# Gate and up products of a feed-forward block, pair by pair in Strassen's scheme

## The chip, the cores and the metric

The kernel runs on one core of one Trainium2 chip. The metric is device time in microseconds (us); the kernel before has a median of 2981.46 us in 3 runs (2981.38 to 2981.63). TensorE (PE) multiplies, VectorE (DVE), ScalarE (ACT) and GpSimd (POOL) do the elementwise work, SyncE (SP) issues the loads of the weights.

## What is computed

Two hybrid layers (convolution, retention, window attention) are followed by one block of another kind, over 512 tokens and a model width of 1024, in float32. The change is in the last stretch of that block:

```
h1 = layer_norm(ALPHA * h + mix)
hid = silu(h1 @ w_ffn_gate) * (h1 @ w_ffn_up)        # 1024 -> 2816, twice
ffn = hid @ w_ffn_down                               # 2816 -> 1024
ple = sigmoid(h1 @ w_ple_gate + b) * (p @ w_ple)
h = layer_norm(ALPHA * h1 + ffn + ple)
```

## The kernel before

Activations lie transposed: 128 features on the partitions, 512 tokens along a row. A float32 product is made of three: each operand is split in a high part (rounded to fp32r) and a low part (the rest), and PE adds high x high, high x low and low x high. Weights come as one stream of slabs of 128x1024, eight tiles of 128x128: for a product of width 1024 the eight tiles that make one tile of 128 outputs. For each slab SP loads it into one of two `raw` buffers, ACT copies it to `whi` (L984, four slots), POOL subtracts in two halves to get `wlo` (L325), and PE makes 8 tiles x 3 terms = 24 matmuls of 512 columns into one bank of `gem` (L392 to L394). POOL's low part frees the raw buffer, PE's last matmul of a slab (`slab_done`) frees the slot.

After the second layer norm (ACT writes the normed rows to `yr`, DVE and ACT the parts `hhi`, `hlo`) comes the per-layer embedding ("PLE"): 8 slabs whose products ACT passes through a sigmoid, and which DVE multiplies by `PL` (L2516) and adds to ALPHA x `yr` in `cv` (L2518).

The feed-forward block has 22 tiles of 128 hidden features in groups of 8, 8 and 6 (`FF_GROUPS`). For each tile the gate slab and the up slab follow each other, a "pair". ACT takes the gate product out of PSUM with Silu (L993), DVE multiplies it by the up product (L2528) and splits the result into `zhi` and `zlo` (L1669 the cast, L1671 the subtraction). After a group come 8 slabs of the down projection (one for each output tile, with as many tiles as the group has pairs), and DVE adds each product to `cv` (L2538). The order of each engine is written out by hand and held together by counting semaphores; every engine executes its own list in order.

## Time and profile before

| | us |
|---|---|
| median of 3 runs | 2981.46 |
| the profiled execution's own time | 2982.7 |
| its span, first to last instruction | 2980.9 |
| PE busy | 2957.1 (99%) |
| DVE, ACT, POOL busy | 1751.4, 1194.3, 1415.5 |

Of PE's 14216 matmuls most have 512 columns. The profile shows 389 ns for one, but they are pipelined, and the distance from start to start tells what they cost. The layer norm before the changed stretch ends near 2577 us, the embedding's slabs near 2607, and the feed-forward matmuls near 2966.

### The profile page before, as it was taken

What the parts mean: (1) busy time and instruction counts of PE and PEld (TensorE: products, weight loads), DVE (VectorE), ACT (ScalarE), POOL (GpSimd) and SP (SyncE); (2) the same over time, 40 slices, a digit from 0 to 9 for tenths busy, and PEclk for the clock granted to TensorE, in tenths of its full rate; (3) what the DMA queues carried; (4) which work ended last, traced back from release to release, by engine and by line L of the source; (5) the groups of instructions that cost most, each with busy time, mean ns of one, the idle gap of its engine ahead of it and who ended that gap; (6) DMA issues with size and microseconds to landing.
All of it is one profiled execution on the core that took longest, in us unless ns stands there. A gap on an engine that the chain in (4) does not pass through costs nothing.

```text
span 2980.9 us, 41951 instructions
## 1 busy us (share of the span) xinstructions
PE 2957.1 (99%) x14216; PEld 2432.5 (82%) x14216; DVE 1751.4 (59%) x2640; ACT 1194.3 (40%) x1820; POOL 1415.5 (47%) x1040
## 2 busy tenths in 40 slices
PE   8999999999999999999999999999999999999998
PEld 6888888878888888888887888888888888788886
DVE  7985677874524598568688644377773343611214
ACT  4233333484332424333347633246553323522223
POOL 5443443455555443443355545544343544554544
PEclk9999999999999999999999999999999999999999
DMA  4322222212223332222221222232222323223222
GB/s 152 99 71 74 95 77 83 88 44 100 92 99 101 121 99 85 85 84 74 81 92 51 86 97 95 97 113 73 76 77 92 107 85 119 94 96 99 98 93 91
DMA packets 73849, 271.06 MB, mean 91 GB/s; under 512 B 8192, under 2 KB 9088, under 8 KB 73088
## 3 DMA queue, kind: packets, MB, share of 16 engines
q1 hardware_dynamic: 70560, 254.84, 26.1%
q10 hardware_dynamic: 3168, 14.61, 1.3%
q8 instruction: 76, 1.25, 0.2%
q14 instruction: 45, 0.37, 0.0%
HBM read 264.17 MB, written 5.24 MB: 90 GB/s over the span
## 4 chain that ended last, share of the span: by engine, by line
PE 86%; issue 7%; POOL 5%; DVE 1%; ACT 1%; DVEq 0%; DMA 0%; POOLq 0%; ACTq 0%; SPq 0%
PE gem L392 19%; PE gem L394 19%; PE gem L393 19%; POOL wlo L325 5%; PE gem L827 2%; PE gem L829 2%; PE gem L828 2%; PE gem L518 2%; PE gem L517 2%; PE gem L519 2%; PE gem L637 2%; PE gem L639 1%; PE gem L638 1%; PE gem L663 1%; PE xp L681 1%
## 5 line engine op out<-in xcount | busy, mean ns | idle before, releaser
L325 POOL TENSOR_TENSOR wlo<-raw,whi 128x512 fp32r<-128x512 f32 x956 | 1320.4, 1403 | 1532.9 <-ACT whi L984 1532.8
L984 ACT ACTIVATE whi<-raw 128x1024 fp32r<-128x1024 f32 x478 | 504.2, 1056 | 667.4 <-PE gem L394 490.8
L392 PE MATMUL gem<-zhi,whi 128*128 128x512 f32 x1664 | 649.1, 390 | 0.3 <-DVE zlo L1671 0.3
L394 PE MATMUL gem<-zhi,wlo 128*128 128x512 f32 x1664 | 647.6, 389 | 0.0
L393 PE MATMUL gem<-zlo,whi 128*128 128x512 f32 x1664 | 647.4, 389 | 0.0
L392 PE MATMUL gem<-hhi,whi 128*128 128x512 f32 x1280 | 498.7, 390 | 0.0
L394 PE MATMUL gem<-hhi,wlo 128*128 128x512 f32 x1280 | 498.0, 389 | 0.0
L393 PE MATMUL gem<-hlo,whi 128*128 128x512 f32 x1280 | 498.0, 389 | 0.0
L392 PEld LDWEIGHTS gem<-zhi,whi 128*128 128x128 f32 x1664 | 312.4, 188 | 65.5 <-DVE zlo L1671 0.8
L394 PEld LDWEIGHTS gem<-zhi,wlo 128*128 128x128 f32 x1664 | 312.3, 188 | 65.3
L393 PEld LDWEIGHTS gem<-zlo,whi 128*128 128x128 f32 x1664 | 312.4, 188 | 64.5
L394 PEld LDWEIGHTS gem<-hhi,wlo 128*128 128x128 f32 x1280 | 240.2, 188 | 50.3
L392 PEld LDWEIGHTS gem<-hhi,whi 128*128 128x128 f32 x1280 | 240.3, 188 | 50.0 <-issue 0.2
L393 PEld LDWEIGHTS gem<-hlo,whi 128*128 128x128 f32 x1280 | 240.3, 188 | 49.8
L993 ACT ACTIVATE U<-gem 128x512 f32<-128x512 f32 x118 | 70.3, 596 | 297.1 <-PE gem L394 271.9
L1887 DVE SCALAR_TENSOR_TENSOR xp<-cv,sm,xp 128x512 f32<-128x512 f32 x224 | 158.6, 752 | 16.2 <-issue 13.9
L993 ACT ACTIVATE U<-gem,vec 128x512 f32<-128x512 f32 x96 | 65.6, 685 | 237.1 <-PE gem L394 215.9
L1826 DVE SCALAR_TENSOR_TENSOR xp<-cv,vec,xp 128x512 f32<-128x512 f32 x208 | 147.8, 752 | 9.0 <-issue 0.4
L2528 DVE TENSOR_TENSOR U<-gem,U 128x512 f32<-128x512 f32 x22 | 15.2, 692 | 185.5 <-PE gem L394 185.5
L827 PE MATMUL gem<-zhi,whi 128*128 128x512 f32 x256 | 106.5, 416 | 0.7 <-POOL wlo L325 0.7
L1993 DVE TENSOR_TENSOR yr<-gem,yr 128x512 f32<-128x512 f32 x64 | 41.2, 685 | 101.8 <-PE gem L394 101.8
L829 PE MATMUL gem<-zhi,wlo 128*128 128x512 f32 x256 | 100.2, 391 | 0.0
(451 smaller groups left out, 4344.9 us busy)
## 6 DMA issues: line engine op xcount, KB each, us to landing
raw<-in_slabs SPq DMA_DIRECT2D x478, 512.0 KB, 3.4
U<-in_x SPq DMA_DIRECT2D x4, 512.0 KB, 6.8
U<-in_x ACTq DMA_DIRECT2D x1, 2048.0 KB, 9.6
xsave<-U ACTq DMA_DIRECT2D x1, 2048.0 KB, 7.1
U<-xsave ACTq DMA_DIRECT2D x1, 2048.0 KB, 9.8
out_y<-yr SPq DMA_DIRECT2D x8, 256.0 KB, 2.2
tab<-in_tab_ret ACTq DMA_DIRECT2D x2, 512.0 KB, 5.1
tab<-in_tab_att ACTq DMA_DIRECT2D x2, 512.0 KB, 3.5
```

Of the source, the lines that this page charges most:

```text
L325: part = pool.tensor_tensor(wlo[:, k % 4, c], raw[:, k % 2, c], whi[:, k % 4, c].bitcast(f32), O.subtract)
L392: pe.matmul(o, wh, hi, start=(n == 0), stop=False)
L393: pe.matmul(o, wh, lo, start=False, stop=False)
L394: mm = pe.matmul(o, wl, hi, start=False, stop=(n == len(terms) - 1))
L517: pe.matmul(o, hhi[:, k, c], wh, start=(k == 0), stop=False)
L518: pe.matmul(o, hhi[:, k, c], wl, start=False, stop=False)
L827: pe.matmul(gem[:, k, :], wh, hhi[:, r, :], start=(r == 0), stop=False)
L829: mm = pe.matmul(gem[:, k, :], wl, hhi[:, r, :], start=False, stop=(r == NT - 1))
L984: act.activation(whi[:, k % 4, :], raw[:, k % 2, :], A.Copy).then_inc(hi_done, 1)
L993: act.activation(dst, gem[:, b, :], func, bias=bias, scale=scale).then_inc(evac[b], 1)
L1826: stt(held if n < TAPS - 1 else TT[:, 0, :], v, w, acc, O.mult, O.add)
L1887: stt(acc if n < TAPS - 1 else TT[:, 0, :], v, w, acc, O.mult, O.add)
```

## The change

The two slabs of a pair are seen as a matrix of 2x2 blocks: A11 and A12 are the gate's four tiles over the lower and the upper half of the 1024 features, A21 and A22 the up slab's. The activations are four blocks too: lower and upper features by the first and last 256 tokens. Strassen's scheme in Winograd's form makes the four block products with 7 multiplications in place of 8. Each is 4 tiles x 3 terms = 12 matmuls of 256 columns, 84 for a pair in place of 48 of 512.

- Weights: DVE makes four sums of 128x512 for each pair (`sums`: S1 = A21 + A22, S2 = S1 - A11, S4 = A12 - S2, S3 = A11 - A21), two pairs ahead of PE. ACT makes the high part of the 7 blocks in half slots of 512 columns, 8 of them; POOL makes the low part of 5 (`BY_POOL`), DVE of S1 and S3 (`low_half`).
- Activations: DVE makes four differences of 128x1024 once, out of `yr` (`lessen`), ACT and DVE split them. ALPHA x `yr` is written to `cv` beforehand, and the embedding adds to it.
- Results: products land in halves of four banks for a pair, alternating between even and odd pairs. Three products each add onto an earlier one in PSUM. ACT copies four halves of 256 tokens out, DVE makes four sums of 256 tokens with one operand in PSUM (`early` makes the gate's first 256 tokens, `late` the rest), ACT applies Silu from SBUF, and DVE multiplies and splits as before.
- PE waits for `early` of a pair before it adds S2 into the bank (`f_added`), for ACT's copies before S4 and S3 (`f_kept`), and for `late` two pairs back before a bank is used again.
- Loads go to four buffers instead of two in this stretch; the down slabs are converted in halves. The loops are written out. DVE makes the sums for a group's first two pairs while the down products of the group before run.

```diff
+N_PLAIN = 4 * (BLOCK_G + PLE) + 10
+PAIRS = sum(FF_GROUPS)
+STARTS = (0, 8, 16)
+A11, A12, S1, A22, S2, S4, S3 = range(7)
+BY_POOL = (A11, A12, A22, S2, S4)
...
+        RAWS = (raw[:, 0, :], raw[:, 1, :], U[:, U_T + 2 * T:U_T + 4 * T], U[:, U_VF:U_VF + 2 * T])
+        flat_tab = tab[:, :, :].rearrange("p a b -> p (a b)")
+        SUM = ((flat_tab[:, 0:T], flat_tab[:, T:2 * T], U[:, U_C:U_C + T], U[:, U_C + T:U_C + 2 * T]),
+               tuple(U[:, U_C + n * T:U_C + (n + 1) * T] for n in range(2, 6)))
+        HALF = T // 2
+        KEPT5, KEPT2 = ([U[:, U_C + (6 + e) * T + n * HALF:U_C + (6 + e) * T + (n + 1) * HALF] for e in range(2)]
+                        for n in range(2))
+        GATE = [U[:, U_SG + (2 + e) * T:U_SG + (3 + e) * T] for e in range(2)]
...
+        DIFF_HI, DIFF_LO = ([quads(t) for t in (
+            Ur[:, at:at + 2 * T], yr_r[:, at:at + 2 * T],
+            yr_r[:, 4 * T + at:6 * T + at], Ur[:, 4 * T + at:6 * T + at])] for at in (0, 2 * T))
+        def half_slot(t, j):
+            n = (4 + j) % 8
+            return t[:, n // 2, n % 2 * T:(n % 2 + 1) * T]
...
-            lows(at, N_SLABS)
+            lows(at, N_PLAIN)
+            def low_half(j, src):
+                pool.wait_ge(f_hi, j + 1)
+                pool.tensor_tensor(half_slot(wlo, j), src, half_slot(whi, j).bitcast(f32), O.subtract).then_inc(f_lo, 1)
+            for g, n in enumerate(FF_GROUPS):
+                for p in range(STARTS[g], STARTS[g] + n):
+                    for m in BY_POOL:
+                        low_half(unit(p, m), source(p, m))
+                for i in range(NT):
+                    for h in range(2):
+                        low_half(unit_out(g, i, h), raw_out(g, i, h))
...
-            m0, z0 = 0, Z0 + 24
-            for n in FF_GROUPS:
-                with pe.Fori(0, n // 2) as it:
-                    for k in range(2, 6):
-                        hslab(Gp + (it + (2 + m0 // 4)), k, up + (it + (4 + m0 // 4)), k0=2)
-                m0 += 2 * n
+            def pair_product(p, m, o, hi, lo, opens=False):
+                j = unit(p, m)
+                if m in BY_POOL:
+                    pe.wait_ge(f_lo, pool_low(p, m))
+                else:
+                    pe.wait_ge(f_own, own_low(p, m))
+                for r in range(4):
+                    wh, wl = (half_slot(w, j)[:, r * P:(r + 1) * P] for w in (whi, wlo))
+                    pe.matmul(o, wh, hi[:, r, :], start=(opens and r == 0), stop=False, skip_group_check=True)
+                    pe.matmul(o, wh, lo[:, r, :], start=False, stop=False, skip_group_check=True)
+                    mm = pe.matmul(o, wl, hi[:, r, :], start=False, stop=(r == 3), skip_group_check=True)
+                mm.then_inc(f_free, 1)
+            def pair(p):
+                g, x, y = p // 8, 2 * (p % 2), 2 * (p % 2) + 1
+                ca, cb, cc, cd = xp[:, x, 0:HALF], gem[:, x, 0:HALF], xp[:, y, 0:HALF], gem[:, y, 0:HALF]
+                t1, t2 = slice(0, HALF), slice(HALF, T)
+                if p >= 2:
+                    pe.wait_ge(f_added, added(p - 2, 2))
+                pair_product(p, A11, ca, hhi[:, 0:4, t1], hlo[:, 0:4, t1], True)
+                if p % 8 < 2:
+                    pe.wait_ge(evac[x], up + 4 + 2 * g + PRIMED)
+                pair_product(p, A12, cb, hhi[:, 4:8, t1], hlo[:, 4:8, t1], True)
+                if p == 0:
+                    pe.wait_ge(f_diff, 9)
+                pair_product(p, S1, cc, DIFF_HI[0], DIFF_LO[0], True)
+                if p % 8 < 2:
+                    pe.wait_ge(evac[y], up + 4 + 2 * g + PRIMED)
+                pair_product(p, A22, cd, DIFF_HI[3], DIFF_LO[3], True)
+                pe.wait_ge(f_added, added(p, 0))
+                pair_product(p, S2, ca, DIFF_HI[1], DIFF_LO[1])
+                pe.wait_ge(f_kept, kept(p, 1))
+                pair_product(p, S4, cc, hhi[:, 4:8, t2], hlo[:, 4:8, t2])
+                pe.wait_ge(f_kept, kept(p, 3))
+                pair_product(p, S3, ca, DIFF_HI[2], DIFF_LO[2])
...
+            def high_half(j, src, arrived):
+                if j >= 8:
+                    act.wait_ge(f_free, j - 7)
+                else:
+                    act.wait_ge(slab_done, N_PLAIN - 4 + j // 2 + 1 + PRIMED)
+                arrived()
+                act.activation(half_slot(whi, j), src, A.Copy).then_inc(f_hi, 1)
...
+                    for m in range(7):
+                        if m == A12:
+                            act.wait_ge(f_free, unit(p, A12) + 1)
+                            if p < 2:
+                                act.wait_ge(sg_used, 8 + PRIMED)
+                            act.activation(GATE[e][:, 0:HALF], gem[:, 2 * e, 0:HALF], A.Copy).then_inc(f_kept, 1)
+                        if m == S1:
+                            act.wait_ge(f_free, unit(p, S1) + 1)
+                            if p >= 2:
+                                act.wait_ge(f_added, added(p - 2, 2))
+                            act.activation(KEPT5[e], y[:, 0:HALF], A.Copy).then_inc(f_kept, 1)
+                        if m == A22:
+                            act.wait_ge(f_free, unit(p, A22) + 1)
+                            if p == 0:
+                                act.wait_ge(f_sum, 4)
+                            else:
+                                act.wait_ge(z_ready, DEPTH * 40 + 24 + p + PRIMED)
+                            act.activation(TT[:, 0, 0:HALF], gem[:, 2 * e + 1, 0:HALF], A.Copy).then_inc(f_kept, 1)
+                        if m == S2:
+                            act.wait_ge(f_free, unit(p, S2) + 1)
+                            act.activation(KEPT2[e], x[:, 0:HALF], A.Copy).then_inc(f_kept, 1)
+                        if m == S3:
+                            act.wait_ge(f_added, added(p, 1))
+                            if p >= 2:
+                                act.wait_ge(z_ready, DEPTH * 40 + 24 + p - 1 + PRIMED)
+                            act.activation(SGB[:, e, :], GATE[e], A.Silu).then_inc(f_kept, 1)
+                        ahead(g, n, 7 * (p - STARTS[g]) + m + 8)
...
+            def lessen(n, x, y):
+                return tt(DIFF[n], x, y, O.subtract)
+            first, second = (slice(n * HALF, (n + 1) * HALF) for n in range(2))
+            lessen(0, yr[:, 0:4, second], yr[:, 0:4, first])
+            lessen(2, yr[:, 4:8, second], yr[:, 0:4, second])
+            dve.drain()
+            lessen(1, yr[:, 4:8, second], DIFF[0]).then_inc(f_diff, 1)
+            dve.drain()
+            lessen(3, yr[:, 4:8, first], DIFF[1]).then_inc(f_diff, 1)
+            for i in range(0, NT, 4):
+                ts(cv[:, i:i + 4, 0:T], yr[:, i:i + 4, :], ALPHA, None, O.mult)
+            dve.drain().then_inc(f_diff, 3)
...
+            def sums(p, ms):
+                a, b = (RAWS[PLACE[load_of(p, n)]] for n in range(2))
+                for m in ms:
+                    if m == S1:
+                        for n in range(2):
+                            loaded(dve, load_of(p, n))
+                        if p >= 2:
+                            dve.wait_ge(f_lo, pool_low(p - 2, S4))
+                        op = tt(sum_of(p, S1), b[:, 0:T], b[:, T:2 * T], O.add)
+                    elif m == S2:
+                        dve.drain()
+                        op = tt(sum_of(p, S2), sum_of(p, S1), a[:, 0:T], O.subtract)
+                    elif m == S4:
+                        dve.drain()
+                        op = tt(sum_of(p, S4), a[:, T:2 * T], sum_of(p, S2), O.subtract)
+                    else:
+                        op = tt(sum_of(p, S3), a[:, 0:T], b[:, 0:T], O.subtract)
+                    op.then_inc(f_sum, 1)
+            def low_half(p, m):
+                j = unit(p, m)
+                dve.wait_ge(f_hi, j + 1)
+                tt(half_slot(wlo, j), sum_of(p, m), half_slot(whi, j).bitcast(f32), O.subtract).then_inc(f_own, 1)
+            def diff_low(at, n):
+                dve.wait_ge(f_dhi, at + 1)
+                tt(DIFF_LO[n], DIFF[n], DIFF_HI[n].bitcast(f32), O.subtract).then_inc(f_diff, 1)
...
-                stt(cv[:, i, 0:T], yr[:, i, :], ALPHA, TT[:, k % 2, :], O.mult, O.add)
+                tt(cv[:, i, 0:T], cv[:, i, 0:T], TT[:, k % 2, :], O.add)
                 dve.drain()
-            m0, z0 = 0, 0
-            for n in FF_GROUPS:
-                with dve.Fori(0, n // 2) as it:
-                    G, u = Gp + (it + (2 + m0 // 4)), up + (it + (4 + m0 // 4))
-                    for k in (3, 5):
-                        product(G, k)
-                        dve.wait_ge(evac[(k - 1) % 4], u + 1 + PRIMED)
-                        j = (k - 3) // 2
-                        tt(TT[:, j, :], gem[:, k % 4, :], SGB[:, j, :], O.mult).then_inc(evac[k % 4], 1)
-                        dve.drain()
-                        split(zhi[:, it * 2 + j, :], zlo[:, it * 2 + j, :], TT[:, j, :], z_ready)
-                        dve.drain()
-                m0 += 2 * n
+                if 4 <= k < 8:
+                    diff_low(k - 4, (0, 3, 1, 2)[k - 4])
+                if k == 7:
+                    sums(0, (S1, S2, S4, S3))
+                if k == 8:
+                    low_half(0, S1)
+            sums(1, (S1, S2, S4, S3))
+            low_half(0, S3)
...
+            def early(p):
+                e = p % 2
+                x = xp[:, 2 * e, :]
+                dve.wait_ge(f_kept, kept(p, 0))
+                tt(GATE[e][:, first], x[:, first], GATE[e][:, first], O.add).then_inc(f_added, 1)
+            def late(p, following):
+                e = p % 2
+                x, y = xp[:, 2 * e, :], xp[:, 2 * e + 1, :]
+                dve.wait_ge(f_free, unit(p, S4) + 1)
+                dve.wait_ge(f_kept, kept(p, 3))
+                tt(GATE[e][:, second], KEPT2[e], y[:, first], O.add).then_inc(f_added, 1)
+                dve.wait_ge(f_free, unit(p, S3) + 1)
+                tt(TT[:, 0, first], x[:, first], TT[:, 0, first], O.add)
+                tt(TT[:, 0, second], x[:, first], KEPT5[e], O.add).then_inc(f_added, 1)
+                if following:
+                    low_half(p + 1, S3)
+                dve.drain()
+                dve.wait_ge(f_kept, kept(p, 4))
+                tt(TT[:, 1, :], TT[:, 0, :], SGB[:, e, :], O.mult)
+                dve.drain()
+                split(zhi[:, p % 8, :], zlo[:, p % 8, :], TT[:, 1, :], z_ready)
+                dve.drain()
+            for g, n in enumerate(FF_GROUPS):
+                last = STARTS[g] + n - 1
+                for p in range(STARTS[g], last + 1):
+                    early(p)
+                    if p + 2 <= last:
+                        sums(p + 2, (S1, S2))
+                    if p + 1 <= last:
+                        low_half(p + 1, S1)
+                    if p + 2 <= last:
+                        sums(p + 2, (S4, S3))
+                    late(p, p + 1 <= last)
```

## Rows read from the trace of the kernel before

**Rows 1.** Page, parts 1 and 2: TensorE's busy time, and its granted clock in 40 slices.
```profile
PE 2957.1 (99%) x14216; PEld 2432.5 (82%) x14216; DVE 1751.4 (59%) x2640; ACT 1194.3 (40%) x1820; POOL 1415.5 (47%) x1040
PEclk9999999999999999999999999999999999999999
```

**Rows 2.** Page, part 4: the chain that ended last, by engine.
```profile
PE 86%; issue 7%; POOL 5%; DVE 1%; ACT 1%; DVEq 0%; DMA 0%; POOLq 0%; ACTq 0%; SPq 0%
```

**Rows 3.** Windows, first pairs: busy us of PE, PEld, DVE, ACT, POOL; granted clock.
```profile
2608.00:2695.00 87.00, 87.00 (x386) 72.03 (x385) 17.98 (x25) 22.44 (x26) 43.76 (x32) 1.00 0.31 100
```

**Rows 4.** Timeline (start us, us, engine, line, operation) of PE, matmuls of 512 columns.
```profile
2694.02 0.39 PE L394 MATMUL gem<-hhi,wlo 128*128 128x512 f32 x1
2696.06 0.39 PE L394 MATMUL gem<-hhi,wlo 128*128 128x512 f32 x1
```

**Rows 5.** Timeline of PE, attention scores, matmuls of 256 columns.
```profile
587.25 0.28 PE L663 MATMUL gem<-zhi,zlo 64*128 64x256 f32 x2
587.72 0.28 PE L663 MATMUL gem<-zlo,zhi 64*128 64x256 f32 x2
```

**Rows 6.** Timeline of PE's weight loads in the HGRN stage.
```profile
2036.84 1.99 PEld L836 LDWEIGHTS xp<-U 128*128 128x128 f32 x16
```

**Rows 7.** Groups by line, shapes apart, 2550 to 2980.9 us: busy us, mean ns, idle before.
```profile
L325 POOL TENSOR_TENSOR wlo<-raw,whi 128x512 fp32r<-128x512 f32 x152 | 208.9, 1394 | 199.1 <-ACT whi L984 199.1
L984 ACT ACTIVATE whi<-raw 128x1024 fp32r<-128x1024 f32 x75 | 79.4, 1058 | 175.8 <-PE gem L394 158.7 <-DMA raw<-in_slabs 16.9 <-PE gem L952 0.2
L993 ACT ACTIVATE U<-gem 128x512 f32<-128x512 f32 x26 | 15.5, 595 | 91.5 <-PE gem L394 91.5
```

**Rows 8.** Timeline of DVE: one pair of the loop before.
```profile
2650.25 0.69 DVE L2528 TENSOR_TENSOR U<-gem,U 128x512 f32<-128x512 f32 x1 [7.78 <-PE gem L394]
2651.13 0.43 DVE L1669 CAST hhi<-U 128x512 f32 x1 [0.19 <-issue]
2651.71 0.69 DVE L1671 TENSOR_TENSOR hlo<-U,hhi 128x512 f32 x1
```

**Rows 9.** Timeline of DVE: gating products of the per-layer embedding.
```profile
2578.99 0.69 DVE L2516 TENSOR_TENSOR U<-U 128x512 f32<-128x512 f32 x1 [3.93 <-ACT U L993]
2579.78 0.69 DVE L2518 SCALAR_TENSOR_TENSOR cv<-yr,U 128x512 f32<-128x512 f32 x1
2580.55 1.63 DVE L2516 TENSOR_TENSOR U<-U 128x512 f32<-128x512 f32 x1
...
2585.66 1.60 DVE L2518 SCALAR_TENSOR_TENSOR cv<-yr,U 128x512 f32<-128x512 f32 x1
```

**Rows 10.** Timeline of POOL beside them, and alone.
```profile
2579.88 6.83 POOL L325 TENSOR_TENSOR wlo<-raw,whi 128x512 fp32r<-128x512 f32 x4 [7.75 <-ACT whi L984]
...
2609.87 2.54 POOL L325 TENSOR_TENSOR wlo<-raw,whi 128x512 fp32r<-128x512 f32 x2 [3.54 <-ACT whi L984]
```

**Rows 11.** Timeline: DVE with a PSUM input (xp) and without, beside POOL.
```profile
2569.13 3.00 POOL L325 TENSOR_TENSOR wlo<-raw,whi 128x512 fp32r<-128x512 f32 x2 [5.67 <-ACT whi L984]
2569.36 0.68 DVE L1728 SCALAR_TENSOR_TENSOR U<-xp,U 128x512 f32<-128x512 f32 x1
2569.97 1.01 DVE L1751 SCALAR_TENSOR_TENSOR zlo<-U,vec,zhi 128x512 fp32r<-128x512 f32 x1
```

**Rows 12.** Groups by line, shapes apart, DVE: a subtraction of 1024 columns.
```profile
L1938 DVE TENSOR_TENSOR hlo<-xp,hhi 128x1024 fp32r<-128x1024 f32 x8 | 9.8, 1225 | 8.8 <-ACT hhi L1161 8.8
```

**Rows 13.** Timeline of PE near the start, around a wait.
```profile
15.65 0.50 PE L477 MATMUL gem<-zhi,whi 128*128 128x512 f32 x1 [1.50 <-DVE zlo L1777]
...
18.24 0.63 PE L477 MATMUL gem<-zhi,whi 128*128 128x512 f32 x1
18.67 0.63 PE L478 MATMUL gem<-zlo,whi 128*128 128x512 f32 x1
```

**Rows 14.** Timeline of ACT: last normed rows, last gate of the embedding.
```profile
2574.18 2.55 ACT L1038 ACTIVATE yr<-U,vec 128x512 f32<-128x512 f32 x4
...
2606.73 0.69 ACT L993 ACTIVATE U<-gem,vec 128x512 f32<-128x512 f32 x1 [3.00 <-PE gem L394]
```

More of the change, by code:

```diff
@@ new lines, in down @@
+            def down(g, n, i):
+                bank = (2 + i) % 4
+                o = gem[:, bank, :]
+                pe.wait_ge(evac[bank], up + 4 + 2 * g + i // 4 + PRIMED)
+                for h in range(2):
+                    j = unit_out(g, i, h)
+                    pe.wait_ge(f_lo, pool_out(g, i, h))
+                    for r in range(4 * h, min(4 * h + 4, n)):
+                        if i == 0:
+                            pe.wait_ge(z_ready, Z0 + 24 + STARTS[g] + r + 1 + PRIMED)
+                        wh, wl = (half_slot(w, j)[:, (r - 4 * h) * P:(r - 4 * h + 1) * P] for w in (whi, wlo))
+                        pe.matmul(o, wh, zhi[:, r, :], start=(r == 0), stop=False)
+                        pe.matmul(o, wh, zlo[:, r, :], start=False, stop=False)
+                        mm = pe.matmul(o, wl, zhi[:, r, :], start=False, stop=(r == n - 1))
+                    mm.then_inc(f_free, 1)
@@ L963, in _ @@
+            for g, n in enumerate(FF_GROUPS):
+                for p in range(STARTS[g], STARTS[g] + n):
+                    pair(p)
                 for i in range(NT):
-                    zslab(Gp + (2 + m0 // 4) + i // 4, 2 + i % 4, up + (4 + m0 // 4) + i // 4,
-                          (z_ready, z0 + PRIMED) if i == 0 else None, n, k0=2)
-                    if z0 + n == Z0 + 24 + sum(FF_GROUPS) and i == 2:
+                    down(g, n, i)
+                    if g == 2 and i == 2:
                         mean_sum(3)
-                m0, z0 = m0 + 8, z0 + n
@@ L1643, in _ @@
                     log_exp()
[L1644 to L1646 removed]
+                for i in range(NT):
+                    for h in range(2):
+                        ahead(g, n, 7 * n + 2 * i + h + 8)
+                    if g == 2:
                         for j in LN_TURNS[i]:
                             centered(3, j, cv[:, j, 0:T])
[L1649 removed]
             shifted_root(3)
```

134 lines of the change are left out of this document (108 added, 26 removed).

## The prediction

> **What bounds the kernel now.** I read the page's busy line first, then the chain, and then the feed-forward stretch by windows, groups and timelines. TensorE is busy 99% of the span at full clock [rows 1], and the chain that ended last is 86% PE work [rows 2]. In the first group of pairs (2608 to 2695 us) PE has no idle time; POOL is busy 43.8 of 87 us, ACT 22.4 and DVE 18.0 [rows 3]. So the stretch costs what PE streams. Nine matmuls of 512 columns start 2.04 us apart [rows 4], 226.7 ns each. A pair (gate slab and up slab) has 48 of them: 10.88 us. Twenty-two pairs are 239.4 us; the down products (about 120 us) stay.
>
> **What it makes of PE.** 7 products x 4 tiles x 3 terms are 84 matmuls of 256 columns per pair. The nearest rows are the attention scores, also split in three terms, 256 columns wide but with 64 rows of the array: four starts span 0.47 us [rows 5], 117.5 ns each. A pair is then 9.87 us, a product 1.41. Below, half of 226.7 ns gives 9.5 us; above, 16 loads of 128x128 weights in a row take 1.99 us [rows 6], 0.124 each, and if loading sets the pace 10.4 us. I take 9.87 because its shape is nearest: 22 x 1.01 = 22 us less, if PE is never kept waiting. The Trainium skill (TensorE: Matmul & The Clock Gate, Back-to-back issue gap) gives N/2.4 + 2.5 ns warm, 109 ns here and 9.2 us a pair; the 512-column row (226.7 against its 216) is slower than that, so I don't use it.
>
> **What it adds elsewhere, per full pair.** POOL: 5 differences of 128x512 instead of 4; alone each takes 1.27 (2.54 for two) [rows 10], 6.35 us of 9.9. ACT: 7 high halves at about 0.6 (1.06 for 1024 columns), 4 copies of 256 at 0.4, one Silu 0.6 [rows 7]: 6.4 us; it fits, but executes in order. DVE had 1.8 us of work in 10.9. Now it has:
> - 8 tensor_tensor of 512 with both inputs in SBUF (4 weight sums, 2 low halves, gate x up, low part of z), 0.69 each alone [rows 8, 9]: 5.52
> - the cast of z: 0.43 [rows 8]
> - 4 sums of 256 with one input in PSUM: 512 columns take 0.69 [rows 8] and 1024 take 1.225 [rows 12], so 256 take 0.42: 1.68
> - 13 gaps after drains and waits, 0.08 to 0.19 in [rows 8, 9], 0.1 taken: 1.3
>
> That is 8.9 us, already 90% of PE's new pair. On top of it comes POOL. When both are busy, DVE's operations with two SBUF inputs take 1.59 to 1.63 instead of 0.69, and POOL's four take 6.83 instead of 5.08 [rows 9, 10]: they alternate, 1.7 us for one of each. With an input in PSUM DVE is not slowed (0.68 beside a running POOL operation), with two in SBUF it is (1.01) [rows 11]. So each POOL operation can cost DVE up to 0.92. The Trainium skill (SBUF — State Buffer, Who interferes with whom) says that a DVE instruction with two SBUF inputs contends with a GpSimd one that reads SBUF, under an exclusive lock; the rows agree, and by this rule the change turns a PE-bound stretch into a DVE/POOL-bound one, which is my forecast.
>
> **One steady pair by hand.** t=0 is the end of product S3 of pair p on PE. DVE: two 256 sums to 0.9. ACT converts A11 of p+2, POOL takes it 0.75 to 1.95; DVE's low half of S3 waits and ends at 2.55. POOL has the next (A12) 2.5 to 3.7; gate x up ends 4.3, cast 4.9, z's low part 5.75; POOL holds 5.7 to 6.9 (A22), beside which early(p+1), with PSUM input, ends at 6.3. Only now may PE start S2 of p+1, for which it was ready at 5.65. Then sums, one low half, two sums and a 256 sum meet POOL's S2 and S4: DVE is through at 12.95, while S2, S4 and S3 on PE ended at 10.5. In the next round ACT's Silu and the highs behind it start late and I get 13.4. The bounds for this cycle T: with no collisions PE's 9.87; with PE kept by early but the rest hidden 6.5 + 4.24 = 10.7; all five collisions at full price 8.9 + 4.6 = 13.5. I take 8.9 + 5 x 0.8 = 12.9 (a collision is cheaper where a PSUM sum lies beside POOL).
>
> **A group.** sums() runs two pairs ahead, so the last two pairs have none. First A11 to early of pair 1: 9.9 + 6.9 = 16.8. Then n-3 cycles of T. Then S2, S4, S3 (4.25) and the tail to the last early (6.9), and 4.25 for the last three products. That is 32.2 + (n-3)T. Over 8, 8 and 6 pairs: 96.6 + 13T = 264.3 at T=12.9, against 239.4: +24.9.
>
> **The start.** DVE gets new work between the layer norm and the pairs. yr is complete at 2576.7 (ACT's last four end there [rows 14]). Then 4 differences of 1024 (1.23 each by [rows 12]) and 2 scalings of 2048 (1.2 each if as fast per element as the cast, 2.3 if not): 7.9 with gaps. Then 8 rounds of 1.58 for the gating, 4 low parts at 1.33, 8 weight sums at 0.79, 2 low halves at 0.8: 25.8. The sum ends at 2610.4 without POOL. POOL runs some 15 operations meanwhile (a pair each 4 to 5.4 us), about 12 us of collisions: 2622.7. PE would need early(0) 5.65 us after the end of the gating products (ACT reads the last at 2606.7 [rows 14]), at 2612.3. So +10, with bounds 0 and 15. ACT is in order too: its read of bank 0 stands behind the high half of S1, which waits for DVE's sums, and PE's A12 waits for that bank.
>
> **The ends of groups.** The down products need the last z 4.8 us (6 pairs: 3.4) after they start; late of the last pair takes about 3.3 + 1.6. +2 in all. Raw tiles come earlier and into 4 buffers; the DMAs have no part in the bound. The old loop's bank traffic hid under PE and its removal gives nothing.
>
> **Sum.** 24.9 + 10 + 2 = +37 on the profiled execution's 2982.7 (span 2980.9 and 1.8 around it); the median of the three runs is 1.2 lower: 2981.5 + 37 = 3018.
>
> **Rivals.**
> - PE stays the bound: if DVE and POOL rarely meet and T is 9.87, the pairs give -22 and the start costs up to 5: 2959 to 2966, 2961 taken. For it: POOL is only 64% busy of such a pair, and its operations are released one by one by products. Against it: DVE's own 8.9 us leave 1 us for five operations of 1.27. It decides below T = 10.1, where 13T - 130.8 crosses zero. By the skill's 109 ns it would be 15 us better still.
> - They collide at half price: the loop through early and S3, T about 10.7, start +6, ends +1: 96.6 + 139 - 239.4 + 7 = +3, so 2985.
> - The clock. The new pair leaves PE idle some 3 us at a stretch. Near the start, 2.6 us after a wait of 1.5 us, matmuls of 512 columns came 0.43 apart [rows 13], the level of 1.2 GHz. A product then costs up to 2.56. If each of the 16 cycles after a group's second pair has such a stretch in S2, S4 and S3, hidden in part, I put 1.5 us on each: +24 on the forecast, 3042. For it: the row. Against it: one idle stretch, at a cold start; in the full cycle DVE's 6.6 us after early cover 4.24 and most of the loss.
>
> **How the numbers follow.** Forecast 65% (its own range T 11.8 to 13.5, start 5 to 15: 2999 to 3033), PE-bound 10%, half price 10%, clock 15%. The range reaches from half price to past the clock: 2986 to 3046. A measurement here can tell 0.2% (6 us) from no change. Faster by more: 0.10. Within: half of the half-price case and a little of the forecast's tail, 0.07. Slower: 0.83.
>
> **What would show it.** PE busy about 80% in the pair stretches, with waits whose releaser is DVE (early, or own low halves). DVE at 90% or more there, its two-SBUF operations at 1.1 to 1.3 mean; POOL's at 1.4 to 1.6. PE 256-column starts 118 ns apart inside a product. Seven-product cycles 12.9 apart in the middle of a group and 11 at its end. PE idle about 10 us around the first pair. I am wrong if PE has no waits on DVE in the pairs, if two-SBUF operations stay near 0.69, or if the 256-column start distance is above 130 ns, where Strassen's scheme gives nothing even with PE alone.

## The result, and the profile after

The kernel before took 2981.42 us (median of 4 runs, 2981.35 to 2981.63), the changed one 3023.76 us (4 runs, 3022.31 to 3025.42): ratio 1.0142, 95% interval 1.0124 to 1.016. The change costs 42 us; 37 were forecast. The profiled execution took 3024.92 us, 42.2 more than the one of before (2982.7).

First the page, parts 1 and 2 (busy us of each engine; granted clock in 40 slices), against [rows 1], then part 4, the chain's shares, against [rows 2]:
```profile
PE 2960.4 (98%) x15008; PEld 2472.8 (82%) x15008; DVE 1968.7 (65%) x2870; ACT 1274.2 (42%) x2046; POOL 1466.5 (49%) x1062
...
PEclk9999999999999999999999999999999999999999
...
PE 78%; issue 7%; DVE 6%; POOL 5%; DVEq 2%; ACT 1%; DMA 0%; POOLq 0%; ACTq 0%; SPq 0%
```
DVE has 217 us more, POOL 51, ACT 80. PE's busy time did not fall (2957.1 before), although each pair streams less: part of its matmuls ran slower (below), which 40 wide slices do not show. The chain has lost eight points of PE, and DVE has gained five.

What PE waited for, over the whole span (engine, line, releaser: us in total, times, longest). The lines of the feed-forward block are L1120 (pairs) and L1161 (down):
```profile
PE xp L1120 <- DVE U L2843: 31.2, 13, 3.0
...
PE xp L1120 <- DVE wlo L2813: 3.6, 1, 3.6
PE gem L1120 <- ACT U L1197: 2.2, 1, 2.2
PE gem L1161 <- DVE hlo L1934: 1.0, 1, 1.0
```
L2843 is `early`: 13 times, up to 3.0 us, PE's S2 stands behind the addition of DVE that frees its bank. That is 31.2 of the 38.0 us that PE waits in the feed-forward block.

Windows of the first pairs and of five pairs inside the second group (busy us of PE, PEld, DVE, ACT, POOL; granted clock; DMA share; GB/s), against [rows 3]:
```profile
2606.16:2731.00 124.84, 104.59 (x742) 99.83 (x741) 98.44 (x111) 56.27 (x110) 74.59 (x51) 0.93 0.29 92
2779.28:2846.34 67.06, 57.84 (x423) 56.82 (x421) 54.84 (x65) 29.67 (x61) 37.00 (x25) 0.87 0.26 79
```
In the second window PE is busy 86%, DVE 82%, POOL 55%, and the granted clock is 0.87: no engine is full. Its pairs start at 2779.28, 2795.13, 2805.45, 2820.18, 2830.5 and 2846.34, so they take 10.3 and 14.7 to 15.9 us in turn. Three of the five are long ones, so their mean of 13.4 us is above the kernel's own. Taken on DVE from one `early` to the next, the 13 cycles between a group's second pair and its last but one take 11.8 to 13.2 us, 12.73 on the mean.

DVE's timeline through one of them (start us, us, engine, line, operation [idle before, releaser]), against [rows 8]:
```profile
2787.69 0.42 DVE L2843 TENSOR_TENSOR U<-xp,U 128x256 f32<-128x256 f32 x1
2788.03 0.68 DVE L2798 TENSOR_TENSOR tab<-raw 128x512 f32<-128x512 f32 x1
2788.81 1.69 DVE L2801 TENSOR_TENSOR tab<-tab,raw 128x512 f32<-128x512 f32 x1
...
2793.70 0.42 DVE L2851 TENSOR_TENSOR U<-U,xp 128x256 f32<-128x256 f32 x1 [1.22 <-PE xp L1122]
2795.33 0.42 DVE L2853 TENSOR_TENSOR U<-xp,U 128x256 f32<-128x256 f32 x1 [1.21 <-PE xp L1122]
...
2796.78 1.61 DVE L2859 TENSOR_TENSOR U<-U 128x512 f32<-128x512 f32 x1
```
POOL's timeline in the same place:
```profile
2788.67 1.27 POOL L512 TENSOR_TENSOR wlo<-U,whi 128x512 fp32r<-128x512 f32 x1 [1.62 <-ACT whi L1830]
```
The operation with two SBUF inputs takes 0.68 alone and 1.69 beside POOL's. In this long pair DVE also waits twice, 1.2 us each, for products that PE did late.

PE's timeline around the first wait for `early` shows why such products are late, against [rows 5] and [rows 13]:
```profile
2606.27 0.28 PE L1121 MATMUL xp<-zlo,whi 128*128 128x256 f32 x1
2606.39 0.28 PE L1122 MATMUL xp<-zhi,wlo 128*128 128x256 f32 x1
...
2623.85 0.58 PE L1120 MATMUL xp<-yr_r,whi 128*128 128x256 f32 x1 [2.78 <-DVE U L2843]
2624.23 0.42 PE L1121 MATMUL xp<-yr_r,whi 128*128 128x256 f32 x1
2624.45 0.41 PE L1122 MATMUL xp<-yr_r,wlo 128*128 128x256 f32 x1
...
2626.79 0.28 PE L1121 MATMUL xp<-zlo,whi 128*128 128x256 f32 x1
2626.91 0.28 PE L1122 MATMUL xp<-zhi,wlo 128*128 128x256 f32 x1
```
Windows, after that wait (same columns as above, granted clock 0.50):
```profile
2624.20:2626.70 2.50, 2.50 (x13) 2.50 (x13) 2.32 (x4) 0.00 (x0) 0.39 (x1) 0.50 0.84 295
```
At full clock 256-column matmuls start 0.12 us apart. After the wait of 2.78 us they start 0.213 apart, the level of 1.2 GHz, and are back at 0.12 by 2626.8. In the block 187 distances are of the slow kind, 187 x 0.094 = 17.5 us of PE time.

A group of POOL and two of DVE, 2570 us to the end (x count, busy us, mean ns, idle before), against [rows 7, 8]:
```profile
L512 POOL TENSOR_TENSOR wlo<-U,whi 128x512 fp32r<-128x512 f32 x82 | 119.7, 1473 | 89.4 <-ACT whi L1830 89.4
...
L2859 DVE TENSOR_TENSOR U<-U 128x512 f32<-128x512 f32 x22 | 36.6, 1663 | 2.0
...
L1932 DVE CAST hhi<-U 128x512 fp32r<-128x512 f32 x23 | 28.5, 1240 | 1.7
```
The product gate x up meets POOL every time (1663 ns against 690), and the cast of z nearly every time (1240 on the mean, 430 alone).

Where the 42 us are: the first pair takes 23.3 us on PE where 9.9 would do (+13.4). The three groups take 280.3 together; without that loss at the start they take 266.9, against 239.4 before (+27.5). The first down product waits 1.0. The sum is 41.9.

### The profile page after: what moved, and what is told of

Its sections match the earlier page's. It is cut to its first block, busy times and chain, and to the rows that moved or that the text cites. A ratio compares the mean times of both kernels' runs of the same rounds, so it can differ in the third digit from the quotient of the medians.

```text
span 3023.1 us, 43745 instructions
## 1 busy us (share of the span) xinstructions
PE 2960.4 (98%) x15008; PEld 2472.8 (82%) x15008; DVE 1968.7 (65%) x2870; ACT 1274.2 (42%) x2046; POOL 1466.5 (49%) x1062
## 3 DMA queue, kind: packets, MB, share of 16 engines
q1 hardware_dynamic: 70560, 254.84, 27.5%
## 4 chain that ended last, share of the span: by engine, by line
PE 78%; issue 7%; DVE 6%; POOL 5%; DVEq 2%; ACT 1%; DMA 0%; POOLq 0%; ACTq 0%; SPq 0%
PE gem L545 14%; PE gem L547 14%; PE gem L546 14%; POOL wlo L465 5%; PE gem L980 2%; PE gem L982 2%; PE gem L981 2%; PE gem L672 2%; PE gem L670 2%; PE gem L671 2%; PE gem L790 2%; PE gem L792 1%; PE gem L791 1%; PE gem L1161 1%; PE gem L1163 1%
## 5 line engine op out<-in xcount | busy, mean ns | idle before, releaser
L465 POOL TENSOR_TENSOR wlo<-raw,whi 128x512 fp32r<-128x512 f32 x820 | 1137.3, 1409 | 1358.1 <-ACT whi L1188 1358.0
L1188 ACT ACTIVATE whi<-raw 128x1024 fp32r<-128x1024 f32 x410 | 432.2, 1056 | 494.3 <-PE gem L547 328.6
L545 PE MATMUL gem<-zhi,whi 128*128 128x512 f32 x1312 | 512.2, 390 | 0.3 <-DVE zlo L1934 0.3
L547 PE MATMUL gem<-zhi,wlo 128*128 128x512 f32 x1312 | 510.8, 389 | 0.0
L546 PE MATMUL gem<-zlo,whi 128*128 128x512 f32 x1312 | 510.6, 389 | 0.0
L545 PE MATMUL gem<-hhi,whi 128*128 128x512 f32 x1104 | 430.3, 390 | 0.0
L547 PE MATMUL gem<-hhi,wlo 128*128 128x512 f32 x1104 | 429.7, 389 | 0.0
L546 PE MATMUL gem<-hlo,whi 128*128 128x512 f32 x1104 | 429.6, 389 | 0.0
L547 PEld LDWEIGHTS gem<-zhi,wlo 128*128 128x128 f32 x1312 | 246.3, 188 | 51.6
L2150 DVE SCALAR_TENSOR_TENSOR xp<-cv,sm,xp 128x512 f32<-128x512 f32 x224 | 158.5, 752 | 16.2 <-issue 13.9
L512 POOL TENSOR_TENSOR wlo<-U,whi 128x512 fp32r<-128x512 f32 x82 | 119.7, 1473 | 89.4 <-ACT whi L1830 89.4
L512 POOL TENSOR_TENSOR wlo<-raw,whi 128x512 fp32r<-128x512 f32 x65 | 98.2, 1524 | 68.0 <-ACT whi L1830 67.9
L980 PE MATMUL gem<-zhi,whi 128*128 128x512 f32 x256 | 106.5, 416 | 0.7 <-POOL wlo L465 0.7
```

Of the source, the lines that this page charges most:

```text
L465: part = pool.tensor_tensor(wlo[:, k % 4, c], raw[:, k % 2, c], whi[:, k % 4, c].bitcast(f32), O.subtract)
L512: pool.tensor_tensor(half_slot(wlo, j), src, half_slot(whi, j).bitcast(f32), O.subtract).then_inc(f_lo, 1)
L545: pe.matmul(o, wh, hi, start=(n == 0), stop=False)
L546: pe.matmul(o, wh, lo, start=False, stop=False)
L547: mm = pe.matmul(o, wl, hi, start=False, stop=(n == len(terms) - 1))
L980: pe.matmul(gem[:, k, :], wh, hhi[:, r, :], start=(r == 0), stop=False)
```

## The experiments

Theory A: DVE and POOL share a resource, and what they do for a pair does not fit into PE's 9.9 us, by the sum of DVE's work and POOL's hold on it. Theory B: the loop through `early` (PE's S3, DVE's work up to `early`, PE's S2) sets the cycle, however much DVE does in all. Theory C: the half clock after waits makes the cost. Theory D: 256-column matmuls are too dear. Where nothing else is said, the edit is to the changed kernel. Each run is compared with runs of the kernel before on the same chip (medians 2981.42 to 2981.54).

**e1_pool_writes: POOL without reads.**
```diff
-                        low_half(unit(p, m), source(p, m))
+                        pool.wait_ge(f_hi, unit(p, m) + 1)
+                        pool.memset(half_slot(wlo, unit(p, m)).bitcast(f32), 0.0).then_inc(f_lo, 1)
```


> POOL writes zeros into the five low parts of a pair in place of subtracting (the low parts of these weight blocks are left out), so it reads nothing from SBUF there; all else is as in the changed kernel (3023.8). If POOL's reads on the shared side are what lengthens DVE's tail (DVE's two-SBUF operations 0.69 in the pairs, early in time), the ten waits of 3 us for early and the half clock after them go: pairs near PE's own 10.1 us, start still 6 to 13 us late, 2974 to 2984. If DVE's own work of 8.9 us or the loop of dependences bounds without POOL: above 3000. If the 256-column matmuls themselves are too slow: no change but the start, above 3010.

Measured 2971.35 us, ratio 0.9968 (0.9955 to 0.998), some 3 us under the range expected. Windows of five pairs:
```profile
2641.00:2690.60 49.60, 48.53 (x411) 48.33 (x410) 33.74 (x56) 29.07 (x59) 19.21 (x26) 1.00 0.35 106
```
DVE's timeline in one of them, then POOL's:
```profile
2642.14 0.69 DVE L2860 TENSOR_TENSOR U<-U 128x512 f32<-128x512 f32 x1
2642.90 0.71 DVE L1933 CAST hhi<-U 128x512 fp32r<-128x512 f32 x1
...
2646.20 0.69 DVE L2814 TENSOR_TENSOR wlo<-tab,whi 128x512 fp32r<-128x512 f32 x1
```
```profile
2642.80 0.53 POOL L518 MEMSET wlo<- 128x512 f32 x1 [0.90 <-ACT whi L1831]
2645.95 0.53 POOL L518 MEMSET wlo<- 128x512 f32 x1 [2.62 <-ACT whi L1831]
```
A pair is 9.92 us, PE is full and its clock 1.00. DVE does all it did, in 6.7 us of 9.9. With POOL not reading, the change gains 10 us instead of losing 42: 52 us hang on its five subtractions. The two-SBUF operation beside a writing POOL (2646.20) keeps its 0.69; the cast does not (0.71 against 0.43).

**e2_small_sums: DVE's four weight sums over 8 columns, POOL untouched.**
```diff
-                        op = tt(sum_of(p, S1), b[:, 0:T], b[:, T:2 * T], O.add)
+                        op = tt(sum_of(p, S1)[:, 0:8], b[:, 0:8], b[:, T:T + 8], O.add)
...
```
S2, S4 and S3 are cut in the same way.

> The four weight sums of a pair are made over 8 of their 512 columns (the rest of S1 to S4 is stale data), which takes about 2.1 us of DVE's work out of each full pair, and their collisions. If DVE's total per pair is the bound: most of the loss goes, 2975 to 2990. If the bound is the way from the end of product S3 through late's tail to early of the next pair, in which no sums stand, the waits for early stay at 2 to 3 us in every second pair and only the start gets shorter: 3008 to 3018.

Measured 2980.89 us, 0.9998 (0.9988 to 1.0007). Between the first and the last of a group pairs take 10.32 us, and the listed waits for `early` are only 3.9 us in all:
```profile
PE xp L1120 <- DVE U L2843: 3.9, 4, 1.1
PE xp L1120 <- DVE wlo L2813: 3.1, 1, 3.1
PE gem L1120 <- ACT U L1197: 1.6, 1, 1.6
```
The loop of theory B has no weight sum in it, and it was untouched, yet the long waits went. So B alone falls: the sum of DVE's work decides when `early` comes, because DVE is in order. But what is left is B's loop: in each of these pairs DVE waits 0.1 us for S3's product and PE 0.3 us for `early`, and the loop closes at 10.32 us. The short pairs of the changed kernel have the same length. By itself, with POOL beside it, the loop costs 0.4 us a pair over PE's 9.92.

**e3_filler: 16 matmuls ahead of the wait for early, to keep PE at work.**
```diff
+                pe.wait_ge(f_kept, kept(p, 0))
+                for r in range(16):
+                    pe.matmul(gem[:, x, t2], ones_r[:, :], hhi[:, 0, t1], start=True, stop=True,
+                              skip_group_check=True)
```


> Before PE waits for early, 16 matmuls of 256 columns go into an unused half bank (1.9 us of extra PE work a pair, 42 us in all). If the half clock after each 3 us wait is a good part of the loss, it goes where the idle time falls near 1 us: S2, S4, S3 take 4.3 in place of up to 7.1, and though pairs without a wait become longer, the total is at most 3025, at best 3010. If the clock is nothing but a by-product of waiting, the filler adds up to 1.9 us in each pair that had no wait: 3035 to 3045.

Measured 3019.34 us (3019.26 to 3019.35), 1.0127 (1.011 to 1.0144): 4.4 us less than the changed kernel, though the filler is 1.9 us a pair (pairs that PE bounds take 11.8 us instead of 9.92). Six pairs in the first group, by windows:
```profile
2627.16:2701.41 74.25, 72.13 (x602) 70.95 (x601) 68.01 (x77) 36.05 (x73) 42.62 (x30) 1.00 0.28 86
```
One cycle of DVE in it, timeline:
```profile
2647.05 0.42 DVE L2847 TENSOR_TENSOR U<-xp,U 128x256 f32<-128x256 f32 x1
2647.39 0.68 DVE L2802 TENSOR_TENSOR tab<-raw 128x512 f32<-128x512 f32 x1
2648.16 1.70 DVE L2805 TENSOR_TENSOR tab<-tab,raw 128x512 f32<-128x512 f32 x1
2649.79 0.68 DVE L2817 TENSOR_TENSOR wlo<-U,whi 128x512 fp32r<-128x512 f32 x1
2650.56 1.61 DVE L2808 TENSOR_TENSOR U<-raw,tab 128x512 f32<-128x512 f32 x1
...
2654.46 1.75 DVE L2863 TENSOR_TENSOR U<-U 128x512 f32<-128x512 f32 x1
2656.29 1.36 DVE L1936 CAST hhi<-U 128x512 fp32r<-128x512 f32 x1
2657.73 1.63 DVE L1938 TENSOR_TENSOR hlo<-U,hhi 128x512 fp32r<-128x512 f32 x1
2659.45 0.42 DVE L2847 TENSOR_TENSOR U<-xp,U 128x256 f32<-128x256 f32 x1
```
The clock is 1.00 and the cycles even: early to early 12.40 us, 2647.05 to 2659.45, and DVE waits for nothing in it: there are six gaps of 0.07 to 0.09 us, and the other operations overlap a little. This is DVE's own time T with POOL beside it. Five of its operations are long, one for each of POOL's: 1.70, 1.61, 1.75 and 1.63 against 0.69, and 1.36 against 0.43. That is 4.86 us, 0.97 each. Theory C can hold for the rest only. The changed kernel's 13 steady cycles, 12.73 us on the mean, are 0.33 longer than this 12.40. The last cycle of a group differs more: 12.8, 13.9 and 14.0 us there, 11.3 here.

**e4_act_keeps: early's place.** ACT copies A11's product away, so that S2 waits for ACT, and early adds A12's product from PSUM.
```diff
-                pe.wait_ge(f_added, added(p, 0))
+                pe.wait_ge(f_kept, kept(p, 0))
+                pe.wait_ge(f_added, added(STARTS[g] + n - 1, 0))
-                            act.activation(GATE[e][:, 0:HALF], gem[:, 2 * e, 0:HALF], A.Copy).then_inc(f_kept, 1)
+                            act.activation(GATE[e][:, 0:HALF], x[:, 0:HALF], A.Copy).then_inc(f_kept, 1)
-                tt(GATE[e][:, first], x[:, first], GATE[e][:, first], O.add).then_inc(f_added, 1)
+                tt(GATE[e][:, first], gem[:, 2 * e, first], GATE[e][:, first], O.add).then_inc(f_added, 1)
```


> ACT copies A11's product (the one that PE adds onto) out of PSUM in place of A12's, and DVE's early adds A12's from PSUM, so that PE's S2 waits for ACT's copy and not for DVE. The computation is the same. If the wait for early is the bound (a dependence, with DVE idle 1.2 and 1.2 us later in the same pair): the 3 us waits go, and T falls from 13.1 to DVE's busy time and gaps, 11.5 to 12: 2998 to 3008. If DVE's total is the bound already: 3016 to 3024.

Measured 3010.21 us, 1.0099 (1.0082 to 1.0116), between the two ranges expected. The wait for `early` is gone, and another has its place:
```profile
PE xp L1120 <- ACT U L1899: 25.6, 15, 2.4
```
PE now waits for ACT's copy of A22, which itself stands behind DVE's last z. Steady cycles are 12.56 us, still DVE without a wait. With DVE full, a wait taken from one product turns up at the next. The 13.5 us gained come with fewer slow matmuls, 91 distances at half clock instead of 187, and lie mostly outside the steady cycles: 4 us in the first pair and more in the last cycles of the groups (9.2 to 10.5 us instead of 12.8 to 14.0).

**e5_before_256: the kernel before, its gate and up slabs in two passes of 256 columns.** The number of matmuls doubles, the columns stay.
```diff
+                        for c in (slice(0, T // 2), slice(T // 2, T)):
+                            for r in range(NT):
+                                o = gem[:, k % 4, c]
+                                pe.matmul(o, wh, hhi[:, r, c], start=(r == 0), stop=False)
...
```


> The kernel before, with the matmuls of the 44 gate and up slabs made in two passes of 256 columns (96 for a pair in place of 48 of 512), nothing else changed. It prices the narrow matmul without any of Strassen's additions: at the 0.118 to 0.120 us of the scores and of the changed kernel's undisturbed products a pair takes 11.3 to 11.5 us in place of 10.88, so 22 pairs add 10 to 14 us: 2991 to 2996. If the narrow matmul is itself a large part of the 42 us (0.13 us each and more with both halves of the weights loaded anew): above 3010.

Measured 2995.67 us (2995.63 to 2995.68), 1.0046 (1.0029 to 1.0063): +14.2 us. Over 22 pairs that is 10.88 + 0.64 = 11.52 a pair of 96 matmuls, 0.120 each. At 0.120 Strassen's 84 take 10.1, and e1's pairs took 9.92. Theory D falls: 0.8 to 1.0 of the 1.01 us a pair are there if PE is never kept waiting.

**e6_all_dve: all seven low parts on DVE, POOL idle in the pairs.**
```diff
-                for p in range(STARTS[g], STARTS[g] + n):
-                    for m in BY_POOL:
-                        low_half(unit(p, m), source(p, m))
...
+                    if p + 1 <= last:
+                        low_half(p + 1, A12)
+                        low_half(p + 1, A22)
...
```


> The changed kernel with all seven low parts of a pair made by DVE, none by POOL (POOL keeps the down slabs). The computation is the same. Theory: DVE is the bound, and a POOL operation costs it about 0.88 us of waiting, more than the 0.77 (operation and gap) of doing it itself. Then T falls from 12.4 (no half clock) to 11.8, and the total from 3024 to 3005 to 3017. Rival: sharing the work with POOL helps, and DVE with 5 x 0.77 = 3.9 us more of its own needs 13 to 15 a pair: 3035 to 3060.

Measured 2983.93 us, 1.0006 (0.9996 to 1.0015): 40 us less than the changed kernel, and far under what I had expected. Windows inside the second group:
```profile
2770.00:2800.00 30.00, 29.26 (x246) 28.85 (x245) 28.54 (x52) 16.88 (x35) 0.00 (x0) 1.00 0.33 104
```
Four lines of DVE's cycle there:
```profile
2775.99 0.69 DVE L2858 TENSOR_TENSOR U<-U 128x512 f32<-128x512 f32 x1
...
2782.96 0.69 DVE L2798 TENSOR_TENSOR U<-U 128x512 f32<-128x512 f32 x1
2783.56 0.69 DVE L2805 TENSOR_TENSOR wlo<-tab,whi 128x512 fp32r<-128x512 f32 x1
...
2786.54 0.69 DVE L2858 TENSOR_TENSOR U<-U 128x512 f32<-128x512 f32 x1
```
The cycle is 10.55 us (2775.99 to 2786.54) with 13 two-SBUF operations instead of 8, and DVE is still the bound (28.54 of 30). Such operations in a row start 0.60 to 0.61 apart, though one lasts 0.69. So DVE's work without POOL's five is 10.55 - 5 x 0.61 = 7.5 us, and a subtraction on POOL costs DVE (12.40 - 7.5) / 5 = 0.98 us, one done by DVE itself 0.61. The expectation had both wrong in the same direction.

**e7_more: e6, and three dependences moved to ACT** (A11's product kept by ACT as in e4; the copy of A22 into a buffer of its own for each parity; the cast of z).
```diff
-                            act.activation(TT[:, 0, 0:HALF], gem[:, 2 * e + 1, 0:HALF], A.Copy).then_inc(f_kept, 1)
+                            act.activation(part[:, e * HALF:(e + 1) * HALF], gem[:, 2 * e + 1, 0:HALF], A.Copy).then_inc(f_kept, 1)
-                split(zhi[:, p % 8, :], zlo[:, p % 8, :], TT[:, 1, :], z_ready)
+                act.activation(Z[DEPTH][0][:, p % 8, :], TT[:, 1, :], A.Copy).then_inc(f_cast, 1)
+                tt(zlo[:, p % 8, :], TT[:, 1, :], zhi[:, p % 8, :].bitcast(f32), O.subtract).then_inc(z_ready, 1)
```


> e6, and three dependences and one operation less on DVE: ACT keeps A11's product so that PE's S2 doesn't wait for DVE; ACT copies A22's product into a place of its own per parity, so that it doesn't wait for the last z; ACT makes the cast of z, DVE only its low part. The computation is the same. If DVE's sum is the bound: 11.8 less 0.43 and a gap, T = 11.3, no long waits and no half clock: 2993 to 3003. If waits in a loop are the bound and not the sum: T near 10.1, 2978 to 2988.

Measured 2971.05 us, 0.9962 (0.9948 to 0.9976), below both ranges expected, which had started from T = 11.8 for e6. Pairs take 9.92 us and PE waits for nothing in them: PE is the bound again, and the scheme pays. DVE's cycle is close behind: 9.88 us in the first group, where it waits for nothing either. What is left are waits at the start (pair 0 takes 13.7, pair 1 12.7).

**e8_shadow: e7, S4's low part on POOL, released so that it lies beside sums with a PSUM input.**
```diff
+                    pool.wait_ge(f_own, own_low(p, S2))
+                    low_half(unit(p, S4), source(p, S4))
```


> e7, with one low part a pair (S4) back on POOL, released when DVE goes over to its three sums with a PSUM input (1.2 us in which DVE doesn't need what they share). If a POOL operation beside PSUM sums is free, T is 0.77 less than in e7, near 10.5 and close to PE's 10.1: 2981 to 2993. If POOL's operation costs DVE as much wherever it lies: as e7 within 3 us or slower.

Measured 2971.10 us, 0.9964 (0.995 to 0.9978), as e7. Since PE is the bound in both, the time tells nothing about what the POOL operation costs DVE there, but the trace does. DVE's timeline, then POOL's:
```profile
2653.21 0.41 DVE L2866 TENSOR_TENSOR U<-xp,U 128x256 f32<-128x256 f32 x1
2653.54 1.02 DVE L2819 TENSOR_TENSOR wlo<-U,whi 128x512 fp32r<-128x512 f32 x1
```
```profile
2652.71 1.30 POOL L513 TENSOR_TENSOR wlo<-U,whi 128x512 fp32r<-128x512 f32 x1 [8.32 <-DVE wlo L2819]
```
The sums with a PSUM input keep their 0.41 to 0.42 us beside POOL, and only the low part behind them is longer, 1.02 instead of 0.68. In the first group, where DVE waits in neither kernel, its cycle is 9.62 us against e7's 9.88. So in this place POOL's subtraction costs DVE 0.33 us, a third of the 0.98 elsewhere and less than the 0.61 of DVE's doing it.

**e9_act_scales: e7, and the residual's two scalings ahead of the pairs by ACT instead of DVE.**
```diff
+                    act.activation(cv[:, i:i + 4, 0:T], yr[:, i:i + 4, :], A.Copy, scale=ALPHA)
-                ts(cv[:, i:i + 4, 0:T], yr[:, i:i + 4, :], ALPHA, None, O.mult)
```


> e7 (2971.1), and ALPHA x yr is written to cv by ACT in two pieces before its first two gate reads, in place of DVE's two scalings (4.5 us of DVE in e7). The computation is the same. Of the 55 us in which DVE works off its new work at the start, PE loses 6 to 7 us around the first two pairs. If DVE's backlog is what PE waits for there, 3 to 4 us of it go: 2966.5 to 2969. If the wait is ACT's order (the high halves stand behind reads that wait for PE), nothing or a loss of up to 2: 2970 to 2973.

Measured 2968.94 us (2968.68 to 2969.08, 5 runs), 0.9957 (0.9943 to 0.9971): the fastest version, 12.6 us under the kernel before. Little of the 2.1 us under e7 lies at the start: the first pair takes 11.3 us instead of 13.7, but the second 14.3 instead of 12.7. Between the two profiled executions (2968.68 and 2971.07), 2.0 of the 2.4 us lie after the last pair. There PE waits 1.9 us in the last group's first down product in e7 and seven 512-column matmuls behind it start 0.43 us apart, the level of 1.2 GHz; in e9 it waits 1.5 us and they start 0.23 apart. The range expected was met, the reason given for it hardly. In the pairs PE waits for this, all near the start but 0.4:
```profile
PE xp L1115 <- ACT U L1888: 2.6, 1, 2.6
...
PE xp L1115 <- ACT U L1899: 0.4, 1, 0.4
```

**e10_waits_only: e7's three edits without e6**, so that POOL keeps its five subtractions (diff as in e7).

> The three edits of e7 without e6: ACT keeps A11's product, ACT copies A22's into its own place, ACT makes the cast of z; POOL makes the five low parts as in the changed kernel. The computation is the same. If the price of POOL's operations (0.98 us of DVE each, from 12.40 with them and 10.55 with DVE's own at 0.61) is the cause by itself: T = 12.4 less 0.43 to 0.9 for the cast, 11.5 to 12, near 3000 (2997 to 3006). If the dependences were the cause and POOL only added to them: within 5 us of e7, 2971 to 2977.

Measured 3000.03 us (2998.0 to 3002.69), 1.0061 (1.0046 to 1.0076). Steady cycles are 11.9 us, from `early` to `early`, and PE waits for ACT's copies that follow DVE:
```profile
PE xp L1121 <- ACT U L1890: 17.4, 14, 2.3
```
DVE is not full in these cycles: it waits 0.97 us in each for ACT's copy, and four of POOL's five operations lengthen its own, by 4.0 us in all. Moving dependences with POOL at work gives 24 us; taking POOL out alone (e6) gives 40, both 53. Of the versions that compute everything, only those in which POOL makes at most one of the five low parts (e6 to e9) come near or under the time of before.

**e11_pool_half: POOL's five over 256 of 512 columns.**
```diff
-                        low_half(unit(p, m), source(p, m))
+                        low_half(unit(p, m), source(p, m), T // 2)
```


> The changed kernel with POOL's five operations in a pair over 256 of the 512 columns (the low parts of the other columns are left as the slot had them). If POOL keeps DVE off for as long as it runs, the price of one falls from 0.98 by about half of 1.0, to 0.45 to 0.5, and T from 12.4 to about 10: PE's 10.1 to 10.4 with few waits, 2977 to 2988. If the price is a fixed one per operation (hand-over), T stays above 11.8: 3005 or more.

Measured 2974.98 us, 0.9978 (0.9969 to 0.9987), a little faster than expected; pairs of 9.92 us between the first and the last of a group. DVE's two-SBUF operation beside the shorter one of POOL:
```profile
2639.60 1.21 DVE L2802 TENSOR_TENSOR tab<-tab,raw 128x512 f32<-128x512 f32 x1
...
2641.50 1.06 DVE L2805 TENSOR_TENSOR U<-raw,tab 128x512 f32<-128x512 f32 x1
```
Beside operations of 0.73 to 1.04 us (1.27 to 1.8 for 512 columns) DVE's last 0.37 to 0.54 longer, 0.43 on the mean of the five in a cycle, not 1.0. The price goes with the length of POOL's operation, not with the number of meetings.

## Why the forecast was right, step by step

The mechanism was the one forecast: DVE and POOL together need more than PE's new pair, and PE waits for `early`. The sign followed. That the total came within 6 us is in part luck: several terms were off, and their errors nearly cancel. The terms:

- **PE's pair, 9.87 forecast.** 9.92 in e1, e7 and e11, 0.118 a matmul; 0.120 by e5. Right. The Trainium skill (TensorE: Matmul & The Clock Gate, Back-to-back issue gap), with N/2.4 + 2.5 ns, would have said 109 ns; the traces do not agree, and the measurement decides.
- **DVE's own work, 8.9 forecast.** 7.5 (e6). Too high by 1.4: I had added 13 gaps of 0.1 us, from operations that follow a drain or a wait. Only six operations of a cycle have such a gap (e3); those in a row have none and even overlap (0.60 apart, 0.69 long).
- **POOL's price, 5 x 0.8 forecast.** 5 x 0.98 (e3 with e6), or 5 x 0.97 read from the long operations of e3; in the changed kernel itself DVE's operations are longer by 4.65 us a cycle, 5 x 0.93. Too low by 0.7 to 0.9: I let the sums with a PSUM input shade some meetings. They do where a POOL operation lies beside them (0.33 us in e8), but in the changed kernel nearly every POOL operation met a DVE operation that it could hold up, the cast of z among them. The Trainium skill (SBUF — State Buffer, Who interferes with whom) says that DVE with two SBUF inputs contends with GpSimd's reads and not with a GpSimd instruction that only writes, and that a cast can contend through its two-port mode. e1 agrees with both: 0.69 beside a memset for the first, 0.71 instead of 0.43 for the cast.
- **T, 12.9 forecast.** 12.73 measured in the changed kernel: 7.6 of DVE's own, 4.65 of POOL's and 0.5 of waits for slow products. 12.40 without such waits (e3). DVE's own work too high by 1.3 to 1.4, POOL's price too low by 0.7 to 0.9 and the waits left out: the near hit is luck.
- **The clock, a rival at 15% with +24.** It came in part. PE's waits of 2 to 3 us were followed by matmuls at 1.2 GHz, as [rows 13] had it. In a long pair DVE then waits up to 2 x 1.2 us for the slow products and comes late with the next sums; with this go the pairs of 10.3 and 13 to 16 us in turn. With T = 12.40 my formula gives 32.2 x 3 + 13 x 12.40 = 257.8 for the groups. Measured are 280.3 - 13.4 (start) = 266.9. The difference is 9.1 us: 4.3 in the 13 steady cycles (0.33 each), 7.3 in the last cycles of the three groups (40.7 us against 33.5 by the formula), and 2.5 less than the formula in their first two pairs. The first two of these I put down to the clock. It is not shown as exactly this: e3 takes most of the half clock away (39 slow distances instead of 187) and its last cycles are 11.3 us, the formula's 11.15, but it adds filler.
- **PE-bound and half price, 10% each.** Neither came as a whole. Steady pairs of 9.92 us appear where POOL does not read (e1), is out or nearly so (e7 to e9) or does half (e11). The loop of the half-price rival, 10.7 us by my sum, exists and takes 10.32 us: it sets the short pairs of the changed kernel and those of e2. The bound of T < 10.1 was too strict: with T at 10.55 (e6) the kernel was even with that of before (1.0006), though 9.8 us were still lost in its first pair. The bound used 32.2 us a group besides the cycles also where PE has little to wait for.
- **The start, +10 forecast.** +13.4. DVE's backlog ends nearly when I had it: `early` of the first pair starts at 2623.4, forecast 2622.7. S2 starts 11.9 us later than PE alone would have it, and S2 and S4 behind the wait ran in part at half clock, which adds the rest. The two scalings take 2.3 us each where I had summed 1.2, but in every run that has them on DVE a POOL subtraction lies beside each and takes 2.3 us too (1.27 alone), so their own time is not shown. The wait of A12 for bank 0 behind ACT, named but not counted, was 2.2 us and is not on the path: PE would have waited for DVE's low half of S1 (3.6) and for `early` (2.8) after it all the same. e9, which takes the scalings out of e7, gains 0.8 us in the first two pairs.
- **The ends, +2 forecast.** One wait of 1.0 at the first down product.
- **What was to show it.** PE busy 84 to 86% (80 forecast) and DVE the releaser: right. DVE at 90% or more: 79 to 82% in the two windows shown, wrong, as its waits for slow products were not foreseen; e3, at full clock, has 92%. Two-SBUF operations at 1.1 to 1.3 mean: 1.12 over the full cycles, from 0.86 (low parts) to 1.66 (the product) by line, so only on the mean. POOL's at 1473 ns (1.4 to 1.6): right. 256-column starts 118 to 120 ns: right. Cycles of 12.9: 12.7 on the mean, but uneven; 11 at a group's end: the last pair takes 11.3 on PE. PE idle about 10 us around the first pair: 8.6.

Where the scheme's gain went: PE's 1 us a pair is real (e1), and the additions that buy it cost DVE more than it had free as long as POOL reads beside it. What stays open is how much of the 9.1 us is the clock, and whether more than one POOL operation a pair could lie beside the PSUM-input sums, where e8's trace shows it at 0.33 us.

## What to carry to other kernels

Price a helper engine's work also by what it takes from the engine beside it: here a subtraction given to POOL cost DVE 0.98 us, and doing it itself 0.61. Look too at where it falls: beside DVE's sums with a PSUM input it cost 0.33. An algorithm that trades matmuls for additions must first find room on the engine that adds; the 12.6 us of e9 came when the helper was taken out and the copies that free the banks were moved to an engine with time. And where PE waited 2 to 3 us here, the products after the wait came at half clock and made the waited-for engine wait in turn.
